# Who makes the low part of a weight unit: GpSimd or VectorE, in the SSD phase of a two-layer encoder

## What is computed

```python
proj = h @ w_in                                   # 1024 -> z, xbc, dt, q_mem
xbc = silu(depthwise_conv_centred(xbc, conv_w, conv_b))
# per head, chunks of 128 tokens, both directions:
y_diag = einsum('bcgrls,bcsgrp->bclgrp', cb * decay_ls, x)
y_off  = einsum('bclgn,bcgrpn,bcgrl->bclgrp', cm, prev, exp(a_cs))
y = rmsnorm((y_fwd + y_bwd + d_skip * xs) * silu(z), norm_g)
x = x + rmsnorm(concat([y, m]) @ w_out, post_g)
```

## Time and profile before

| | |
|---|---|
| median of three runs | 2145.84 us (2143.32 to 2146.58) |
| span of the profiled execution | 2143.2 us (its own time is not shown apart) |
| TensorE (PE) busy | 2099.4 us, 98% |
| VectorE (DVE) busy | 1089.1 us, 51% |
| GpSimd (POOL) busy | 924.6 us, 43% |
| ScalarE (ACT) busy | 800.1 us, 37% |
| L188, rounding, 217 times | 245.9 us, mean 1133 ns |
| L191, low part, 217 times | 550.6 us, mean 2537 ns |

### The profile page before, as it was taken

One profiled execution on the slowest core, in us unless ns is written; L12 is line 12 of the kernel. 1 busy time (PEld: TensorE's weight loads), 2 busy tenths in 40 slices (PEclk: granted clock), 3 DMA queues, 4 the chain that ended last, 5 costly groups with the idle time before them and its releaser, 6 DMA issues.

```text
span 2143.2 us, 31195 instructions
## 1 busy us (share of the span) xinstructions
PE 2099.4 (98%) x12580; PEld 1789.7 (84%) x12580; DVE 1089.1 (51%) x1866; ACT 800.1 (37%) x1943; POOL 924.6 (43%) x623
## 2 busy tenths in 40 slices
PE   8999999999999999999999999999999999999997
PEld 7888887788898888787788887888888888888885
DVE  4104332598898898897712233144333423541447
ACT  4123122465464555473322111143424323432343
POOL 5533332333343343325742332654454445544544
PEclk9999999999999999999999999999999999999999
DMA  5221112335232233235331111322131223123213
GB/s 189 90 68 53 51 50 74 137 98 143 80 109 80 70 118 100 78 119 173 125 125 50 50 50 50 96 87 68 59 88 59 68 59 96 40 68 86 69 50 118
DMA packets 206685, 184.19 MB, mean 86 GB/s; under 512 B 23916, under 2 KB 172684, under 8 KB 206541
## 3 DMA queue, kind: packets, MB, share of 16 engines
q1 hardware_dynamic: 206541, 182.20, 27.7%
HBM read 168.19 MB, written 12.21 MB: 84 GB/s over the span
## 4 chain that ended last, share of the span: by engine, by line
PE 50%; DVE 4%; issue 1%; ACT 0%; DMA 0%; POOL 0%; DVEq 0%; POOLq 0%; ACTq 0%
PE bank L214 25%; PE bank L264 9%; PE bank L574 6%; PE bank L2411 2%; PE bank L2439 2%; PE bank L1067 2%; PE bank L2422 2%; PE bank L1093 1%; DVE acc L944 1%; PE bank L1131 1%; DVE acc L940 1%; DMA R<-macc_dram 0%; PE bank L447 0%; DVE R L422 0%; PE bank L2483 0%
## 5 line engine op out<-in xcount | busy, mean ns | idle before, releaser
L188 POOL TENSOR_SCALAR Wh<-Wraw 128x1024 fp32r<-128x1024 f32 x217 | 245.9, 1133 | 1100.2 <-issue 755.2
L214 PE MATMUL bank<-Hh,Wh 128*128 128x512 f32 (+1 forms) x1936 | 664.6, 343 | 3.2 <-ACT R L817 1.4
L214 PE MATMUL bank<-Hl,Wh 128*128 128x512 f32 (+1 forms) x1936 | 652.0, 337 | 0.0
L214 PE MATMUL bank<-Hh,Wl 128*128 128x512 f32 (+1 forms) x1936 | 651.0, 336 | 0.0
L191 POOL TENSOR_TENSOR Wl<-Wraw,Wh 128x1024 fp32r<-128x1024 f32 x217 | 550.6, 2537 | 18.1
L214 PEld LDWEIGHTS bank<-Hh,Wh 128*128 128x128 f32 x1936 | 367.7, 190 | 51.0 <-issue 10.8
L214 PEld LDWEIGHTS bank<-Hh,Wl 128*128 128x128 f32 x1936 | 367.3, 190 | 39.0
L214 PEld LDWEIGHTS bank<-Hl,Wh 128*128 128x128 f32 x1936 | 367.9, 190 | 36.6 <-issue 1.7
L298 DVE TENSOR_TENSOR acc<-bank,acc 128x512 f32<-128x512 f32 x240 | 165.0, 690 | 166.3 <-PE bank L264 165.5
L264 PE MATMUL bank<-Wh,Mh 128*128 128x512 f32 x528 | 208.7, 395 | 8.7 <-DVE acc L298 7.6
L264 PE MATMUL bank<-Wh,Ml 128*128 128x512 f32 x528 | 205.7, 390 | 0.0
(11 more groups left out here) (259 smaller groups left out, 3124.0 us busy)
## 6 DMA issues: line engine op xcount, KB each, us to landing
Wraw<-in_na_w_in_dram SPq DMA_DIRECT2D x80, 512.0 KB, 3.8
Wraw<-in_ssd_w_in_dram SPq DMA_DIRECT2D x57, 512.0 KB, 4.2
Wraw<-in_w_out_dram SPq DMA_DIRECT2D x48, 512.0 KB, 3.3
R<-acs_dram SPq DMA_DIRECT2D x16, 1536.0 KB, 6.8
Wraw<-in_w_mem_kv_dram SPq DMA_DIRECT2D x32, 512.0 KB, 3.9
R<-gs_dram SPq DMA_DIRECT2D x32, 128.0 KB, 3.5
R<-R SPq DMA_DIRECT2D x32, 128.0 KB, 3.6
macc_dram<-acc SPq DMA_DIRECT2D x1, 3072.0 KB, 11.5
```

Of the source, the lines that this page charges most:

```text
L188: pool.tensor_scalar(Wh[:, s, :], Wraw[:, s, :], 1.0, 1.0, ALU.mult, ALU.mult).then_inc(pool_c, 1)
L214: mm = pe.matmul(DB[h.k % 2][:, 0:t1 - t0], w[:, k, :], x[:, k, t0:t1], start=(k == 0 and i == 0), stop=(k == KC - 1 and i == 2))
```

## The change

`split_unit` stays for all units but 47 of the SSD phase (indices 6 to 52). For those GpSimd runs `high_unit`: it waits for the load and for `unit_done` as before, rounds `Wraw` to `Wh` and raises a new semaphore `high_split`. It no longer subtracts. VectorE runs `low_unit`: it waits for `high_split` and for the low part before it, subtracts and raises `w_ready`. The 47 calls of `low_unit` are written into VectorE's order of the loop: between the two operations of the segment (steps 1 to 14), ahead of `backward` (steps 1, 3, 5, 7, 9 and the even steps from 2), ahead of the output evictions (even steps 2 to 12), behind the first tap inside the second half of those evictions, and at the end of the first block of taps in odd steps (once) and in step 0 (twice).

```diff
+        def high_unit(pool):
+            u = U["pool"]
+            s = u.k % 2
+            pool.wait_ge(raw_landed[s], u.base * 8 + 16 * (u.k // 2 + 1))
+            pool.wait_ge(unit_done, u.value + 1)
+            settle(pool)
+            pool.tensor_scalar(Wh[:, s, :], Wraw[:, s, :], 1.0, 1.0, ALU.mult, ALU.mult).then_inc(high_split, 1)
+            u.next()
+
+        def low_unit(dve):
+            u, highs = U["low"], U["high"]
+            s = u.k % 2
+            highs.next()
+            dve.wait_ge(high_split, highs.value)
+            dve.wait_ge(w_ready, u.value + 2)
+            dve.tensor_tensor(Wl[:, s, :], Wraw[:, s, :], Wh[:, s, :].bitcast(F32), ALU.subtract).then_inc(w_ready, 1)
             u.next()
...
+            FIRST_LOW, END_LOW = 6, unit_index(LAST) - 1
...
-                for _ in range(unit_index(PAIRS) - 4 + 2):
-                    split_unit(pool)
+                for u in range(4, unit_index(PAIRS) + 2):
+                    if FIRST_LOW <= u < END_LOW:
+                        high_unit(pool)
+                    else:
+                        if u == END_LOW:
+                            pool.wait_ge(w_ready, U["pool"].value + 2)
+                        split_unit(pool)
...
+                        if 0 < n < LAST:
+                            low_unit(dve)
                         dve.tensor_tensor(seg, seg, ab[:, 1, :, :].rearrange("p h (c l) -> p c h l", l=P), ALU.min)\
...
                     if group_unit(n):
                         conv5(j, n + 1, dense)
+                    if n and group_unit(n) or out_in(n):
+                        low_unit(dve)
 
                     backward(n)
...
+                    if out_in(n) and n < LAST - 1:
+                        low_unit(dve)
...
                         for half in range(2):
-                            dve_out(dve, (half,), first=(n == 2), then=lambda k: tap(j, n + 1, 2 * half + k) if n < LAST else None)
+
+                            def then(k):
+                                tap(j, n + 1, 2 * half + k)
+                                if (half, k) == (1, 0):
+                                    low_unit(dve)
+
+                            dve_out(dve, (half,), first=(n == 2), then=then)
                     elif n < LAST:
                         if not group_unit(n):
                             conv5(j, n + 1, dense)
                         if n:
                             low_part(n - 1)
+                        for _ in range(2 if n == 0 else 1):
+                            low_unit(dve)
```

More of the change, by code:

```diff
@@ L139, in encoder_kernel @@
         raw_landed = [sem("raw_landed0"), sem("raw_landed1")]
-        w_ready, unit_done = sem("w_ready"), sem("unit_done")
+        w_ready, unit_done, high_split = sem("w_ready"), sem("unit_done"), sem("high_split")
         half_done, dense_free = sem("half_done"), sem("dense_free")
@@ L145, in encoder_kernel @@
         dve_c, act_c, pool_c = sem("dve_c"), sem("act_c"), sem("pool_c")
-        U = {k: Count() for k in ("sp", "pool", "pe", "act", "dve")}
+        U = {k: Count() for k in ("sp", "pool", "pe", "act", "dve", "low", "high")}
         HF, HD = ({k: Count() for k in ("pe", "act", "dve")} for _ in range(2))
@@ L1730, in vector @@
                 dve.wait_ge(pre.cst[2], 32)
+                U["low"].k = unit0 + FIRST_LOW
                 def low_part(n):
@@ L1888, in vector @@
                                           ALU.add).then_inc(reduced, 1)
+                assert U["low"].k == unit0 + END_LOW
                 HF["dve"].k = half0 + 2 * dense_index(PAIRS)
```

## The result

The changed kernel takes 2162.59 us (median of 4 runs, 2160.91 to 2163.87); the kernel before, run beside it, 2144.58 us. The ratio is 1.0085, with an interval of 1.0071 to 1.0098: 18.0 us slower. The forecast was 2164.4 us, 18.6 us above the kernel before. The profiled execution took 2160.91 us, with a span of 2158.1 us.

What follows compares the result with a forecast made beforehand. TensorE was taken to bound the kernel, busy 100.00 of 100 us in mid-phase. Terms 5.4 + 2.0 + 7.2 + 2.8 + 1.2 = +18.6 us gave a 2161.8 us span and 2164.4 us median; range 2152 to 2177.

Steps and rivals of the forecast that it cites:

- Relief: VectorE operations with two SBUF inputs: each GpSimd subtraction removed gives back 2.2 us where it met one.
- Step 0: TensorE's third unit, unit 6: waits 7.1 us for its low part; a later 1.7 us wait goes; net +5.4 us.
- Clock: After the step 0 pause: TensorE runs part of its work at half clock, +2 us, between 0 and 3.4.
- Even steps 4 to 10: Low parts ahead of and inside the output evictions make TensorE wait, 1.8 us together, four steps: +7.2 us.
- Step 2: VectorE reaches the evictions 1.9 us later after standing still for unit 10's load; in-loop place 0.9: +2.8 us.
- Steps 11 to 14: VectorE already late; units 44 and 50 come 0.5 and 2.85 us late, older waits shrink or go: sum +1.2 us.
- Queues: Loads and GpSimd's new waits: cost 0 with the cover, up to 4 us per unit where it fails.
- The signs: Step 0 pause some 7 us, 47 low parts of 1.2, L1803 down about 1, eviction waits, TensorE idle up about 16.
- Rival A: Only step 0 costs, as VectorE's relief is larger and it reaches evictions 1 us earlier: +7.4, 2153; chance 0.18.
- B: Smaller relief, and waits for high parts halt VectorE: each even step costs 2.7 + 0.9, 2175; chance 0.15.
- C: Faster: 7.5 us of waits from late VectorE vanish and low parts come in time, 2138; chance 0.03.
- D: No change: the 7.1 us are real, 7.5 us come back, evictions cost nothing, 2146; chance 0.04.

Runs made afterwards that it cites:

- the moved low parts: Low parts of units 10, 44 and 50 placed behind a second tap, against the version with unit 6 and the 12 eviction units back on GpSimd: 2137.14 us.

## Why the prediction was right

The mechanism was right: an exchange that is even on VectorE, one long wait in step 0, the clock behind it, and two places of every output projection without slack. The sizes were right less closely than the total suggests. Matched matmul by matmul, the terms come to 16.0 us where the forecast had 18.6, all but the clock and the wait of step 0 being smaller than forecast; that the medians lie 18.0 us apart is closer to the forecast than its terms were.

- *Price.* 1.22 us measured, 1.2 taken. 57.5 us of new work.
- *Relief.* L1803 over 768 columns fell by 0.64 us on the mean, where I had said about 1: 22 of its 32 operations had run at 0.95 us in the kernel before, untouched by GpSimd. The sum was right: VectorE's total busy time is 1.3 us lower. The prediction said that by the rule on the port pair alone all 47 low parts would be cheaper on VectorE. They are not: the 12 at the evictions cost 12.5 us there by the medians and 10.0 by the traces, because TensorE's slack and not VectorE's load decides at that place. The section of the Trainium skill ("SBUF — State Buffer", section "SBUF: two separate sides") does not promise it either: outside VectorE's faster modes it names only VectorE operations with two SBUF inputs, and an eviction has one input in PSUM. That the subtraction does hold VectorE's two-input operations back, as that section has it, is shown by the kernel in which both engines subtract.
- *Step 0.* The wait is 7.79 us, of which 0.65 had been there for ScalarE: 7.1 new ones, as forecast. The wait of 1.69 us for L1821 is gone, as forecast.
- *Clock.* 10.8 - 8.6 = 2.2 us, forecast 2. The number came out by luck: the forecast let the clock fall 4.5 us into the pause and stay low for 6.9 us. In the trace the mean was 0.93 over the first 3 us of the pause and 0.50 right behind them, and the clock was full again only between 437.9 and 440.9, so that the low stretch lasted some 10 us. It fell earlier and lasted longer, and about 5 us of it lay on work where 4.3 had been forecast.
- *Even steps 4 to 10.* 0.49 to 0.53 and 0.85 us of idle time, with the bubble beside it 0.65 to 0.7 and 1.0; forecast 0.8 to 0.95 and 0.9. In step 6 the first eviction comes 0.85 us later in TensorE's order of work than before, where I had reckoned 1.0.
- *Step 2.* Waits of 2.02 and 0.86 us stand where one of 0.93 stood: +2.1 with the bubbles, forecast 2.8. VectorE stood still for the load of unit 10 for 2.46 us, as the forecast had it (2).
- *Steps 11 to 14.* The waits for units 44 and 50 are 1.09 and 2.72 us, forecast 0.5 and 2.85. The wait of 2.43 us in step 12 shrank to 0.71, more than the 0.9 that I gave it; the sum is slightly below zero instead of +1.2 (and the forecast's own terms add up to 1.1).
- *Queues.* No row of the changed kernel has TensorE waiting for a load. The loads do come later at two places (GpSimd waits 20.65 us for that of unit 50 in step 13), but the moved low parts show that this was covered.
- *The signs.* They came as named but for two sizes: L1803's mean fell by 0.64 us and not by about 1, and TensorE's idle rows in the phase grew by 13.0 us and not by about 16: with the bubbles the waits cost 13.8 us and the clock 2.2.

From the start of step 0 to the end of the phase the changed kernel takes 16.0 us more by its trace; the medians lie 18.0 us apart, with an interval of 15.2 to 21.0. Where the other 2 us are is not shown. Rival A (only step 0 costs) fails by the evictions, which cost 10 us or more alone; B by their size, 0.65 to 0.7 and 1.0 us instead of 2.7 and 0.9; C at the point that it had named, the start of unit 6; D by the evictions, which it had at nothing.

## What to carry to other kernels

Work may go to a busy engine for nothing, if it takes away what had stopped that engine, and still cost time: count the exchange over a step, then look at each place for the slack of the engine that bounds, since 1.2 us at a place with 0.2 us of slack are lost whatever the sum says. When work becomes part of another engine's fixed order, check the first round of a loop apart: the unit that is consumed in the same round has to be made ahead of its consumer. And measure the version that leaves the moved work out: it told here that no placing in the present order of work could bring more than about 12.3 us, and how near the moved version (7.7) had come.

## What the runs showed that I had not expected

In the kernel where both engines make the low part, 47 more GpSimd subtractions of 2.4 us (113 us of work on an engine that is 37% busy) cost 83 us; by the trace 28.6 us of it are TensorE's own matmuls, at a lower mean clock. And behind one pause of 7.8 us TensorE paid 2.2 us on the next unit, with the clock at its lower level until some 5 us into that unit.
